# Two modulation steps moved ahead of the grouped attention, and the queries' deviations moved into the softmax's scale

## The reference

```python
def second_block(x, c, ada_w, ada_b, ...):
    c_act = jax.nn.silu(c)
    for i in range(DEPTH):
        mod = c_act @ ada_w[i] + ada_b[i]          # 1024 x 6144
        sh1, sc1, g1, sh2, sc2, g2 = jnp.split(mod[:, None, :], 6, axis=-1)
        h = x * (1 + sc1) + sh1
        y = neighbourhood_mixer(h, ...) if i % N_MIXERS == 0 else gqa_mixer(h, cos, sin, ...)
        x = layer_norm(DEEPNORM_ALPHA * x + (1 + g1) * y, ln_g[i, 0], ln_b[i, 0])
        h = x * (1 + sc2) + sh2
        y = hierarchical_moe(h, ...)               # 32 experts, 2 per token
        x = layer_norm(DEEPNORM_ALPHA * x + (1 + g2) * y, ln_g[i, 1], ln_b[i, 1])

def gqa_mixer(h, cos, sin, w_qkv, q_gain, k_gain, w_o):   # 16 query heads, 4 key heads
    q = apply_axial_rope(rms_norm(q, q_gain), cos, sin)
    k = apply_axial_rope(rms_norm(k, k_gain), cos, sin)
    return block_gqa_attention(q, k, v) @ w_o             # softmax(q k / 8) v
```

## Time and profile before

| | us |
|---|---|
| median of 3 runs | 1565.1 |
| lowest, highest | 1564.13, 1570.44 |
| the profiled execution | 1563.89 |
| its span, first to last instruction | 1562.2 |
| TensorE busy | 1389.6 (89%) |
| VectorE busy | 571.8 (37%) |
| ScalarE busy | 215.0 (14%) |
| GpSimd busy | 88.4 (6%) |
| mean granted clock of TensorE | 0.949 |

### The profile page before, as it was taken

How to read it: one execution, slowest core, us unless ns; L and a number is a source line. 1 busy time by engine, 2 the same in 40 slices (tenths; PEclk the granted TensorE clock), 3 DMA queues, 4 the chain that set the end, 5 groups by cost and what they waited for, 6 DMA issues and landing times.

```text
span 1562.2 us, 28408 instructions
## 1 busy us (share of the span) xinstructions
PE 1389.6 (89%) x12800; PEld 883.6 (57%) x12800; DVE 571.8 (37%) x1254; ACT 215.0 (14%) x574; POOL 88.4 (6%) x95
## 2 busy tenths in 40 slices
PE   7999999999998999779879788878999797897795
PEld 4885478578886556346446344457655453463451
DVE  3696469655745111101101115684222011011013
ACT  2230123022332000000000002442100000000000
POOL 3100111000003000000000001100200000000000
PEclk9999999999999999889899898999999998998997
DMA  9656845768768999999999998257999999999995
GB/s 345 216 197 233 291 164 198 275 220 288 280 278 340 411 426 426 428 426 426 427 426 428 427 376 320 89 201 282 374 413 426 428 426 427 427 426 427 425 415 201
DMA packets 96856, 533.32 MB, mean 341 GB/s; under 512 B 5184, under 2 KB 7424, under 8 KB 73168
## 3 DMA queue, kind: packets, MB, share of 16 engines
q1 hardware_dynamic: 92992, 519.40, 82.6%
q0 software_dynamic: 3728, 11.95, 2.2%
HBM read 530.28 MB, written 1.05 MB: 340 GB/s over the span
## 4 chain that ended last, share of the span: by engine, by line
PE 65%; DMA 24%; DVE 4%; SPq 4%; ACT 1%; issue 1%; DVEq 0%; ACTq 0%
PE bk L433 28%; PE bk L898 16%; DMA ring<-in_moe_w_down 15%; DMA AR<-in_moe_w_down 9%; PE bk L932 8%; PE bk L614 4%; PE bk L942 4%; SPq L2325 3%; PE bk L429 3%; DVE AR L1017 2%; PE bk L643 1%; PE bk L658 1%; ACT AR L1831 1%; DMA ring<-in_w_in 1%; DVE AR L1025 0%
## 5 line engine op out<-in xcount | busy, mean ns | idle before, releaser
L898 PE MATMUL bk<-ring,AR 128*32 128x128 f32 x4480 | 268.6, 409 | 0.1
L1017 DVE TENSOR_TENSOR AR<-bk,AR 128x128 f32<-128x128 f32 (+2 forms) x106 | 41.3, 390 | 521.6 <-ACT AR L1831 455.6
L898 PE MATMUL bk<-AR 128*32 128x128 f32 x3712 | 223.0, 409 | 0.0
L898 PEld LDWEIGHTS bk<-ring,AR 128*32 128x32 f32 x4480 | 175.7, 127 | 80.9 <-DVE X L1017 4.5
L433 PE MATMUL bk<-ring,AR 128*128 128x256 f32 (+2 forms) x736 | 214.1, 449 | 6.3 <-ACT AR L1831 2.6
L932 PE MATMUL bk<-ring,AR 128*32 128x512 f32 x608 | 159.4, 704 | 51.9 <-DMA ring<-in_moe_w_down 51.1
L1831 ACT ACTIVATE AR<-bk 128x512 f32<-128x512 f32 (+4 forms) x178 | 72.1, 422 | 948.2 <-PE bk L898 774.1
L898 PEld LDWEIGHTS bk<-AR 128*32 128x32 f32 x3712 | 145.5, 127 | 68.5 <-DVE X L1017 4.5
L433 PEld LDWEIGHTS bk<-ring,AR 128*128 128x128 f32 x736 | 140.9, 194 | 73.7 <-issue 56.6
L932 PE MATMUL bk<-AR 128*32 128x512 f32 x416 | 150.9, 709 | 27.8 <-DMA AR<-in_moe_w_down 27.8
L433 PE MATMUL bk<-AR,ring 128*128 128x256 f32 (+1 forms) x832 | 170.5, 364 | 1.7 <-DVE AR L1022 1.4
(11 more groups left out here) (152 smaller groups left out, 954.1 us busy)
## 6 DMA issues: line engine op xcount, KB each, us to landing
ring<-in_moe_w_gate SPq DMA_DIRECT2D x36, 2048.0 KB, 28.6
ring<-in_moe_w_up SPq DMA_DIRECT2D x34, 2048.0 KB, 25.0
ring<-in_moe_w_down SPq DMA_DIRECT2D x34, 2048.0 KB, 33.6
AR<-in_moe_w_up SPq DMA_DIRECT2D x30, 2048.0 KB, 29.9
AR<-in_moe_w_gate SPq DMA_DIRECT2D x28, 2048.0 KB, 26.3
ring<-in_ada_w SPq DMA_DIRECT2D x24, 2048.0 KB, 11.0
AR<-in_moe_w_down SPq DMA_DIRECT2D x22, 2048.0 KB, 33.6
ring<-in_w_in SPq DMA_DIRECT2D x12, 2048.0 KB, 12.6
```

Of the source, the lines that this page charges most:

```text
L898: ins = eng.matmul(o[32 * f:32 * f + 32, 128 * m:128 * m + 128], XG[u][:, c, 32 * j:32 * j + 32], w[:, c, f::4], start=c == 0, stop=c == N ...
L1017: return eng.tensor_tensor(o, a, b, op)
```

## The change

- Tile 0's steps move to the start of layer 0, before VectorE's scaling of "cq", and eight further steps are done in each first layer: layer 0 now has tiles 0 to 6, layer 1 tiles 7 to 14, the neighbourhood attention 15 to 21 and the grouped attention 22 and 23. In layer 1 four of the added steps stand behind "a0" and four behind "a1". Each first layer has one sum and one extraction more.
- `LOADS`: in layer 0 the first modulation tile is loaded ahead of "qk"; each layer loads one tile more. GpSimd waits for "qk" instead of "cq" before it issues its second set of small loads. silu(c) moves up on ScalarE's list.
- Two accumulators up to tile 14, four from 15 on.
- The queries are no longer multiplied by their deviations. The variance of a unit is scaled by 64, so that the power yields deviation / 8; it goes into the scale operand of the exponential and into the negated maximum. The deviations get places of their own (`RQ`). The order of the grouped attention's side list is tightened.

```diff
-FILL = tuple((("qk0",), ("qk1",) + one, ("v0",), ("v1", "tot"), ("s0",), ("s1", "Sd"), ("a0",), ("a1", "Sc", "Sa"),
-              ("b1", "tot"), ("b0",), ("g1", "tot"), ("g0",), ("spat", "tot", "Sb")) for one in ((), ("tot",)))
+FILL = tuple((("qk0",), ("qk1", "tot"), ("v0",), ("v1", "tot"), ("s0",), ("s1", "Sd"), ("a0",), ("a1", "Sc", "Sa"),
+              ("b1", "tot"), ("b0",) + one, ("g1", "tot"), ("g0",), ("spat", "tot", "Sb")) for one in ((), ("tot",)))
-MIX_SIDE = tuple(((), one, (), ("ext", "v1"), (), (), ("s1", "svar", "ada", "bd"), ("a0", "svn", "ada"),
-                  ("a1", "ada"), ("b1", "z", "ext", "ada"), ("b0", "conv", "ada"), ("g1", "su", "ext", "ada"), ("g0",),
-                  ("spat", "gb")) for one in ((), ("ext",)))
+MIX_SIDE = tuple(((), ("ext",), (), ("ext", "v1"), (), (), ("s1", "svar", "ada", "bd"), ("a0", "svn", "ada") + half,
+                  ("a1", "ada") + half, ("b1", "z", "ext", "ada"), ("b0", "conv") + one + ("ada",),
+                  ("g1", "su", "ext", "ada"), ("g0",), ("spat", "gb")) for half, one in (((), ()), (("ada",), ("ext",))))
-LOADS = (("cq", "qk", "v", "ada", "s", "a", "ada", "b", "ada", "g", "ada", 0, "ada", 1, "ada"),
-         ("cq", "ada", "qk", "v", "ada", "s", "a", "ada", "b", "ada", "g", "ada", 0, "ada", 1, "ada"))
+LOADS = (("cq", "ada", "qk", "v", "ada", "s", "a", "ada", "b", "ada", "g", "ada", 0, "ada", 1, "ada"),
+         ("cq", "ada", "qk", "v", "ada", "s", "a", "ada", "ada", "b", "ada", "g", "ada", 0, "ada", 1, "ada"))
...
-GQA_ROUNDS = (("q01",), ("r10",), ("q11",), ("r01",), ("t21",), ("r11",),
-              ("o00",), ("l", "o01"), ("o02", "t22"), ("o03",))
-GQA_SIDE = (("x20", "v10"), ("w10",), ("v01", "+", "w01"), ("+",), ("v11", "+", "w11"), ("+",), ("x21", "n", "+"), ("m", "+", "o00"),
-            ("l", "o01"), ("o02", "x22", "o03", "s"))
+GQA_ROUNDS = (("q01",), ("r10",), ("q11",), ("r01",), (), ("r11",), ("o00",), ("l", "o01"), ("o02",), ("o03",))
+GQA_SIDE = (("x22", "v10", "w10"), ("+",), ("v01", "w01"), ("+",), ("v11", "w11"), ("n", "m"), (), ("o00",),
+            ("l", "o01"), ("o02", "o03", "s"))
...
         def part(n):
-            return PART[n % 2 if n < 13 else (n - 11) % 4]
+            return PART[n % 2 if n < 15 else (n - 13) % 4]
...
                     extract(next(n_tot))
-                    ada(8)
+                ada(8)
                 v.wait_ge(*filled("in", l, "cq", 1))
...
-                        v.tell(ts(nm, m, -sc, ALU.mult), sem("nm"), nth(tag, p))
+                        if tag == "gqa":
+                            v.wait_ge(sem("grs"), ROPED.index(g["unit"]) + 1)
...
+                            v.tell(stt(nm, m, -1.0, rs, ALU.mult, ALU.mult), sem("nm"), nth(tag, p))
+                        else:
+                            v.tell(ts(nm, m, -sc, ALU.mult), sem("nm"), nth(tag, p))
...
-                    v.wait_ge(sem("grs"), n + 1)
-                    v.step(tt(x, x, bcast(st2[:, 8 * (n % 2):8 * (n % 2) + nh], 2, 64), ALU.mult))
+                    if f[0] == "k":
+                        v.wait_ge(sem("grs"), n + 1)
+                        v.step(tt(x, x, bcast(st2[:, 8 * (n % 2):8 * (n % 2) + nh], 2, 64), ALU.mult))
...
-                                      scale=g["scale"] if plain else 1.0, accum_out=sm[:, u, 8 + a:9 + a])
+                                      scale=g["rs"][:, ORDER[a]:ORDER[a] + 1] if plain else 1.0, accum_out=sm[:, u, 8 + a:9 + a])
...
-            g.wait_ge(*loaded("in", 0, "cq"))
+            g.wait_ge(*loaded("in", 0, "qk"))
             layer_loads(0)
```

More of the change, by code:

```diff
@@ L86 @@
+GQA_LOADS = ((2, 14), (0, 39), (1, 52), ("ada", 22, 8), ("ada", 23, 50), ("wo", 0, 115), ("wo", 1, 123))
 ROPED = ("k0", "k1", "q00", "q10", "q01", "q11")
@@ L241, in program @@
         QKV = BF[:, 0:3072].rearrange("p (t n) -> p t n", t=NT)
+        RQ = [[st2[:, 16 + 16 * t + 8 * j:24 + 16 * t + 8 * j] for t in range(NT)] for j in range(2)]
         GQT = BF[:, 3072:5120].rearrange("p (b n) -> p b n", b=8)
@@ L1540, in variance @@
                     v.chain()
[L1541 removed]
+                    k = 64 if f[0] == "q" else 1
+                    v.tell(ts(ss, ss, k / 64, ALU.mult, k * EPS, ALU.add), sem("gvar"), n + 1)
                 def rotate(f):
                     n, t, nh, x = heads(f)
[L1545 to L1546 removed]
+                    if f[0] == "k":
+                        v.wait_ge(sem("grs"), n + 1)
+                        v.step(tt(x, x, bcast(st2[:, 8 * (n % 2):8 * (n % 2) + nh], 2, 64), ALU.mult))
                     v.chain()
@@ L1653, in router @@
                 v.tell(eng.tensor_copy(cnt[:, NE:NE + 1], rt(388, 1)), sem("cnt"), i + 1)
-                for n in (23,) if i else (18, 19):
+                for n in (23,) if i else (20, 21):
                     extract(n)
@@ L1886, in first_layer @@
                 even_columns("xT", l, ng[:, l])
+                if not l:
+                    s.wait_ge(sem("in"), 80)
+                    s.tell(act(ccol[:, :], ccol[:, :], ACT.Silu), sem("silc"), 1)
                 s.wait_ge(*filled("in", l, "cq", 0))
```

32 lines of the change are left out of this document (15 added, 17 removed).

## The result

The changed kernel takes **1582.4 us** (median of 4 runs, 1581.6 to 1584.5) where the kernel before took 1565.7 us beside it (4 runs, 1564.1 to 1570.4): a ratio of 1.0104, 95% interval 1.0079 to 1.0128, **slower by 1.0%**. It lies in the range (1566 to 1585) and 2.4 us above the forecast's upper edge (1572 to 1580). The profiled execution took 1582.7 us, span 1581.0.

What follows compares the result with a forecast made beforehand. TensorE's in-order list was taken to bound the first layers and attentions, weight loads the expert stages. Terms -8.2 + 7.9 + 9.1 + 3.4 = +12.2 us gave 1577 us, forecast 1572 to 1580, range 1566 to 1585.

Steps and rivals of the forecast that it cites:

- Grouped attention, -8.2: Grouped attention: less VectorE and TensorE work ends waits, but new ScalarE waits of 2.1 and 2.6 us appear; -8.2 us.
- The waits named: Grouped attention: TensorE's waits of 2.03 us before the fourth group, 5.87 for bank 7 and 0.87 before the router's sums go.
- The 2.57 us wait: Grouped attention: TensorE's wait at 1001.89 us for ScalarE's copy stays; the q11 product behind it runs 8.83 us.
- First layer, +7.9 and 1.7 of clock: First layer: late deviation +5.6 us, one more sum 0.87, its bank +1.4; low clock of 1.7 us behind the wait.
- Landing, deviation, wait and the 1.37 us for the bank: First layer: q/k lands at 23.1 us, deviation ready at 32.9, TensorE waits 5.6 us, v product waits 1.37 for its bank.
- Second layer, +9.1 and 1.7 of clock: Second layer's attention: added steps make TensorE wait 2.8 and 3.1 us, plus small items and a sum; low clock 1.7 us.
- the small items: Second layer: 0.6 us for the bank of the next scores and 1.1 us for group 3's normalisation.
- The neighbourhood attention keeps its seven tiles; only their numbers change: Neighbourhood attention: renumbering its modulation tiles costs nothing, 0 us.
- The expert stages pass a shift on unchanged: Both expert stages: the weight stream starts when TensorE lets it, so earlier shifts arrive whole at the end; 0 us themselves.
- three signs of being wrong: Small loads leaving GpSimd before 20 us, VectorE idling nowhere in the second layer's attention, or expert stages changing their length.
- The clock, +3.4 and inside the grouped term -1.8: Low clock of 1.7 us each behind the first layer's wait and one second-layer wait; grouped attention regains 1.8 us.
- Rival 3: Front and grouped attention: q/k lands nearer 28.9 us, new waits keep the clock low; +3 to +9 us, chance 0.14.

Runs made afterwards that it cites:

- scale or tiles alone: Scale: only the queries' deviations moved, on the kernel before, 1564.7 us, ratio 0.9998. Tiles: that part undone in the changed kernel, 1588.9 us, one execution.
- the second half: The changed kernel with only layer 1's four added steps behind a1 moved to the end of its side list: 1574.6 us, ratio 1.0055.
- The moved extractions: The changed kernel with the sums and extractions of tiles 18 and 19 moved later in the neighbourhood attention: 1583.1 us, ratio 1.0124.
- both halves late: The changed kernel with both groups of four added steps of layer 1, and one sum with its extraction, moved late in its side list: 1576.9 us, ratio 1.0069.
- that run: The kernel before with only GpSimd's two layer norm additions put behind VectorE's gate multiplication: 1561.6 us, ratio 0.9960.
- the mended change: The changed kernel with mends of the first layer, layer 1, neighbourhood attention and GpSimd's additions: 1562.8 us, ratio 0.9987; with layer 1 set differently 1564.2 us, ratio 0.9977.

## Why the prediction was right or wrong

**The sign and the sum were right, for the most part by its own steps.** The medians moved by 16.7 us for the 12.2 forecast; what is missing is in stages that it had at nothing. To judge each step by itself I took the clock out of each stage: over slices of 2.5 us the length times (1 - granted clock), summed.

| stage | before, full clock + loss | change, full clock + loss | full clock | clock |
|---|---|---|---|---|
| l=0 | 148.2 + 1.7 | 155.6 + 5.1 | +7.4 | +3.4 |
| l=1 | 154.7 + 1.7 | 161.4 + 3.4 | +6.7 | +1.7 |
| neighbourhood attention | 134.6 + 0.0 | 135.9 + 1.7 | +1.3 | +1.7 |
| grouped attention | 103.5 + 10.9 | 98.8 + 6.4 | -4.6 | -4.6 |

- *Grouped attention, -8.2*: measured -9.2. The waits named went, those for ScalarE came. But only half is work and waits; the clock term, taken at 1.8 us, is 4.6, and it moves: kernels with the same lists there lost 3.4, 6.4 and 9.3 us to the clock. The 2.57 us wait "stays": it does (2.92), but the product behind it took 7.13 us, not 8.83. Over nine profiles with these lists it is 6.7 us in the mean, over five with other ones (before, scale or tiles alone) 11.0.
- *First layer, +7.9 and 1.7 of clock*: +7.4 and +3.4. Landing, deviation, wait and the 1.37 us for the bank each came within 1.2 us. How the sum splits is less sure here than elsewhere: over the profiles of unchanged front code the stage takes 148.2 to 151.0 us, over those of changed code 159.6 to 160.8, with clock losses that partly fall into waits. Whole it is +10.5 in the mean for +9.6 predicted.
- *Second layer, +9.1 and 1.7 of clock*: +6.7 and +1.7. Mis-sized were the small items, 1.7 us predicted (0.6 and 1.1), 0.17 measured; by the experiments the second half costs 3.0 us of the layer's 6.7. One pair of profiles is a weak base here: over six profiles with this list the layer takes 164.8 to 166.9 us, with 161.4 to 162.6 of it at full clock, over four with the list of before 154.7 to 156.4. Whole it is +10.5 in the mean for +10.8 predicted.
- *"The neighbourhood attention keeps its seven tiles; only their numbers change"*: **this step failed**, +3.0. The number of a tile says what its extraction is. Numbers 16 and 17 are gate rows of one instruction (0.70 us), 18 and 19 need two and three (1.75 and 1.94). They now fall in rounds 4 and 5, on VectorE's list just ahead of the maxima. The moved extractions show it for 1.4 us of wait. The 1.7 us of clock beside it come with that wait in seven profiles of seven (above). Six of the seven profiles with this list take 137.6 us (with both halves late it is 139.8), all four with that of before 134.6.
- *The expert stages pass a shift on unchanged*: **failed**, +5.1 in the profile, 3.5 of it the hit of GpSimd's additions on the first experts. That the expert stages change their own length was one of the prediction's three signs of being wrong, and it came. It isn't a price of the change's steps alone: the kernel before has it in part of its executions, which may be why the medians differ by 16.7 us and the profiles by 18.8. The last 1.6 us, in the second experts' stage, are mostly this profile's: the stage takes 480.2 to 481.5 us in the eight other profiles with the change's grouped attention, and 480.5 to 481.3 in three of the four of kernels made on the one before (the fourth was hit).
- *The clock, +3.4 and inside the grouped term -1.8*: +6.8 and -4.6. One of two waits of the second layer was to pay. Over all profiles low clock came behind the first layer's pair of waits in six of six, behind the second layer's wait of 2.63 us in four of seven and behind its 3.24 us in six of six, twice as much as counted in five of these. The Trainium skill says in "TensorE: Matmul & The Clock Gate", Part 1, that "the default state is throttled, and activity releases the throttle". The traces agree in part: low clock comes behind waits here, but neither that sentence nor my count tells behind which. The waits of 2.92 and 2.60 us in the grouped attention cost nothing in this profile, and of seven equal waits of 0.45 or 0.46 us two were followed by low clock and five weren't.
- *Rival 3* (1580 to 1586, chance 0.14) named the time that came, by mechanisms that did not: q/k landed at 24.2 us, not 28.9, and the new waits of the grouped attention kept no low clock in this profile (behind the last of them it came in three others of the nine).
- *Luck.* Over all profiles with the same lists the three stages come to +10.5, +10.5 and -7.9 us, together +13.1 for +12.2, but errors cancel within two of them: the second layer is +7.1 at full clock and +3.4 of clock for 9.1 and 1.7 predicted, the grouped attention -4.4 and -3.5 for -6.4 and -1.8. That the time stayed in the range, with the neighbourhood attention and the experts unforeseen, is the range's width.

## What to carry to other kernels

Renumbering work that goes round in a list isn't free: look up what each number costs (extraction, bank, buffer) and who stands behind it, and expect that one entry more shifts every later bank. Ask of each load that is moved on a queue which computations stand behind its issue; moving those ahead won 8 us here, and issuing the loads early again only 3, since the weights then landed 5.5 us later. Take two parts of a change apart before you credit one, and take the clock out first: here they were worth 1.7 and 3.5 us alone and 4.6 together, while by their lengths it was nothing, 3 and 9. And give a mend that doesn't belong to the change to the kernel before as well: without that run the mended change would have passed for a gain.

## What the runs showed of the hardware

- **GpSimd's running instruction holds VectorE's.** Two VectorE multiplications of 128x128 with both inputs in SBUF take 0.48 us together with GpSimd idle. Where the first begins while GpSimd runs a two-input instruction, it ends 0.15 us after that one does, in all 26 such pairs of the 14 profiles, whether GpSimd multiplies (X<-AR) or adds (X<-X,AR). Where that was a multiplication the pair took 0.9 to 1.7 us: what was left of it was short, and the second of the pair took its usual 0.28 us. Once the first addition has begun (4.7 us for two), the second of the pair waits for the second addition, and the pair takes 4.3 to 4.8 us. A copy out of a bank isn't held: 0.42 us at 499.95 in the kernel before, with the additions running, and 0.42 at 527.02 in the changed one, without. "GPSIMD Engine Reference" of the Trainium skill, section 8, says that GpSimd shares its SBUF interfaces with VectorE, with contention for instructions with two SBUF inputs. The trace agrees on who is hit, and adds the size: the small one waited for the end of the large one. The second layer seems to have it too, which nobody tested: the four modulation steps of 5.11 us in the earlier trace rows, which left VectorE no slack there, began with two two-input instructions of GpSimd beside them, and four such steps alone take 3.12 us (at 262.86 in the changed kernel). GpSimd in the kernel before:

```profile
241.91 2.94 POOL L2186 TENSOR_TENSOR AR<-AR 128x512 f32<-128x512 f32 x2 [6.66 <-DVE AR L1022]
```

- **Low clock costs equal pieces.** In the three stages ahead of the experts the loss by the table's method was 0, 1.7, 3.4 or 5.1 us, to 0.1, in all but one (4.9) of the 42 stages of the 14 profiles. In l=1 with the code of the kernel before what is left is the same in four profiles (154.66 or 154.67 us), while its length is 154.7 or 156.4. It isn't so everywhere: in l=1 of the changed list 161.4 to 162.6 us are left over six profiles. Stages of the same code differ by whole pieces, which no edit in them explains. A profile pair that differs by 2 us in such a stage shows nothing until this is taken off.
